# Weight panels signalled in quarters, second output panels begun early, the latent-attention sums moved behind the values

## What is computed

```python
# block 1
h = rmsnorm(x, norm_mix_g); proj = h @ w_in           # many column groups
ya = (sigmoid(mo) * head_rmsnorm(mlstm(...))) @ w_br_m
yb = head_rmsnorm(diff_attention(...)) @ w_br_d
x = x + (sigmoid(g_a) * ya + sigmoid(g_b) * yb) @ w_out
x = x + (gelu(gt) * val) @ w_down                       # val, gt: conv(rmsnorm(x) @ w_up)
x = x + sigmoid(rmsnorm(x) @ w_ple_gate) * (p @ w_ple)
# block 2, layer 0: stick-breaking attention, 16 heads of 64
x = x + (silu(gate) * stick_breaking(q, k, v)) @ l0_w_out
# block 2, layer 1: latent attention, 8 heads of 128 + 64
q, k = rms over 192 (nope | rope) of each head, from a q latent of 256 and a kv latent of 128
x = x + (silu(gate) * causal_softmax(q k^T) v) @ l1_w_out
# block 3: FFN, gated unit | forgetting attention, 8 heads of 64, FFN; modulated by c @ w_ada
y = (norm_a(u * spatial_gate(v)), norm_b(forgetting_attention(...))) @ w_out_3
```

## Time and profile before

| | |
|---|---|
| median of 3 runs | 2626.04 us |
| profiled execution, its own time | 2632.99 us |
| span in the trace | 2631.0 us |
| TensorE busy | 94%, mean granted clock 0.973 |
| VectorE, ScalarE, GpSimd busy | 50%, 39%, 38% |
| DMA | 245.52 MB, mean 93 GB/s |

### The profile page before, as it was taken

How to read it: one execution, slowest core, us unless ns; L and a number is a source line. 1 busy time by engine, 2 the same in 40 slices (tenths; PEclk the granted TensorE clock), 3 DMA queues, 4 the chain that set the end, 5 groups by cost and what they waited for, 6 DMA issues and landing times.

```text
span 2631.0 us, 31263 instructions
## 1 busy us (share of the span) xinstructions
PE 2477.1 (94%) x11720; PEld 1987.5 (76%) x11720; DVE 1324.2 (50%) x1870; ACT 1023.2 (39%) x1327; POOL 1007.3 (38%) x758
## 2 busy tenths in 40 slices
PE   7999899899999899998988899999989989999999
PEld 5887677688887678776766678888869657688886
DVE  6456667866667661444446662222373544522224
ACT  5445576422222543665446542222253433322222
POOL 3332244445554443222443244444424104344442
PEclk9999899999999999999989999999989998999999
DMA  3221496222222122101221122222212102122221
GB/s 137 81 75 54 167 365 261 103 96 96 96 96 96 66 84 75 49 33 50 95 96 64 35 84 96 99 99 98 96 57 93 49 17 80 48 97 96 98 99 57
DMA packets 35957, 245.52 MB, mean 93 GB/s; under 512 B 3951, under 2 KB 4079, under 8 KB 7188
## 3 DMA queue, kind: packets, MB, share of 16 engines
q1 hardware_dynamic: 30096, 207.12, 21.9%
q10 hardware_dynamic: 5764, 37.06, 3.7%
HBM read 242.06 MB, written 2.11 MB: 93 GB/s over the span
## 4 chain that ended last, share of the span: by engine, by line
issue 55%; POOL 28%; PE 15%; DVE 1%; DVEq 0%; POOLq 0%; ACT 0%; ACTq 0%
POOL WL L286 28%; PE PS L316 5%; PE PS L318 5%; PE PS L317 5%; PE PS L1030 0%; PE PS L377 0%; DVE X L2429 0%; DVE ARENA L2424 0%; POOLq L290 0%; DVEq L2095 0%; DVE ARENA L1771 0%; DVEq L2428 0%; PE PS L382 0%; DVE ARENA L1746 0%; POOLq L283 0%
## 5 line engine op out<-in xcount | busy, mean ns | idle before, releaser
L286 POOL TENSOR_TENSOR WL<-WT,WH 128x512 fp32r<-128x512 f32 x754 | 1007.1, 1367 | 1587.9 <-ACT WH L1054 1069.4
L316 PE MATMUL PS<-HH,WH 128*128 128x512 f32 x1568 | 623.2, 397 | 33.8 <-POOL WL L286 10.3
L317 PE MATMUL PS<-HL,WH 128*128 128x512 f32 x1568 | 615.7, 393 | 0.0
L318 PE MATMUL PS<-HH,WL 128*128 128x512 f32 x1568 | 615.6, 393 | 0.0
L1386 ACT CAST WH<-WT 128x2048 fp32r<-128x2048 f32 x90 | 171.9, 1910 | 603.8 <-PE PS L316 603.8
L316 PEld LDWEIGHTS PS<-HH,WH 128*128 128x128 f32 x1568 | 297.7, 190 | 110.4 <-DVE HL L1780 14.6
L316 PE MATMUL PS<-YH,WH 128*128 128x512 f32 x840 | 334.1, 398 | 24.6 <-DVE YL L2559 6.6
L318 PEld LDWEIGHTS PS<-HH,WL 128*128 128x128 f32 x1568 | 297.5, 190 | 63.6
L317 PEld LDWEIGHTS PS<-HL,WH 128*128 128x128 f32 x1568 | 297.9, 190 | 59.6 <-issue 0.2
L318 PE MATMUL PS<-YH,WL 128*128 128x512 f32 x840 | 329.9, 393 | 0.0
L317 PE MATMUL PS<-YL,WH 128*128 128x512 f32 x840 | 329.8, 393 | 0.0
(11 more groups left out here) (305 smaller groups left out, 3350.8 us busy)
## 6 DMA issues: line engine op xcount, KB each, us to landing
WT<-weights SPq DMA_DIRECT2D x188, 1024.0 KB, 4.8
ARENA<-w_ada ACTq DMA_DIRECT2D x33, 1024.0 KB, 6.8
ARENA<-w_ada SPq DMA_DIRECT2D x3, 1024.0 KB, 7.6
X<-x_fm SPq DMA_DIRECT2D x4, 512.0 KB, 7.3
out_fm<-X SPq DMA_DIRECT2D x8, 256.0 KB, 2.1
ARENA<-rel_rows ACTq DMA_DIRECT2D x1, 1024.0 KB, 5.2
CON<-constants SPq DMA_DIRECT2D x1, 640.0 KB, 11.2
WT<-weights SPq DMA_DIRECT2D x1, 512.0 KB, 5.1
```

Of the source, the lines that this page charges most:

```text
L286: i = nc.gpsimd.tensor_tensor(WL[s][:, e], WT[s][:, e], WH[s][:, e].bitcast(F32), ALU.subtract)
L316: i0 = nc.tensor.matmul(o, w[0], r[0], start=first, stop=False, skip_group_check=True)
L317: nc.tensor.matmul(o, w[0], r[1], start=False, stop=False, skip_group_check=True)
L318: i2 = nc.tensor.matmul(o, w[1], r[0], start=False, stop=last, skip_group_check=True)
```

## The change

Four edits in the order of the program.

1. GpSimd signals after each of the four pieces: three times `w_piece`, the last time `w_lo`. In most places outside the feed-forward blocks TensorE opens a panel with `open_pieces` (waits for the cast alone) and waits for a piece in front of the first matmul that reads it. The first matmul of a panel signals `w_used` as before, so the next cast may come earlier. The feed-forward blocks and the panels inside the differential and forgetting attentions keep `open_panel`.
2. The second output panel of the stick-breaking layer (G_OUT2 + 1) and of block 3 (G_OUT4 + 1) is accumulated in PSUM banks that the attention no longer uses (4 and 5; 2 and 3), by `ahead_steps`. ScalarE casts that panel earlier, and VectorE reads these two tiles from there.
3. In latent attention TensorE does `mla_sums` and `mla_spread` behind the values of the turn; ScalarE does `mla_root` behind the copy.
4. VectorE does `mla_keys` at j = 1 and `mla_out` behind tile j = 0, with `mla_diag` in the middle of it.

```diff
@@ GpSimd, low
-                i.then_inc(sem("w_lo"), 1)
+                    i.then_inc(sem("w_lo" if c + PANEL // 4 == width else "w_piece"), 1)
@@ TensorE
+            def open_pieces(g):
+                pe.wait_ge(sem("w_hi"), g + 1)
+                opened.update(g=g, piece=0)
+                return g
+            def piece(g, end):
+                if opened["g"] == g and end > PANEL // 4 * opened["piece"]:
+                    q = (end - 1) // (PANEL // 4)
+                    opened["piece"] = q + 1
+                    if q == 3:
+                        pe.wait_ge(sem("w_lo"), g + 1)
+                    else:
+                        pe.wait_ge(sem("w_piece"), 1 + 3 * (g - 1) + q + 1)
@@ exact3 (part = panel, end column, weights are the moving operand)
                 i0 = nc.tensor.matmul(o, w[0], r[0], start=first, stop=False, skip_group_check=True)
+                if part and part[2]:
+                    piece(part[0], part[1])
                 nc.tensor.matmul(o, w[0], r[1], start=False, stop=False, skip_group_check=True)
+                if part and not part[2]:
+                    piece(part[0], part[1])
                 i2 = nc.tensor.matmul(o, w[1], r[0], start=False, stop=last, skip_group_check=True)
@@ raw_panel, panel_h, v_panel, out_gemm, the third merge panel, G_PLE, G_MLV
-                open_panel(g)
+                open_pieces(g)
@@
+            def ahead_steps(g, c, b, k0, k1, frees=False):
+                for k in range(k0, k1):
+                    i0, i2 = exact3(psb(b), wtile(g % 2, 8, 256, k, c, c + P), (YH[:, k, :], YL[:, k, :]), k == 0, k == DT - 1,
+                                    (g, k * 256 + c + P, False))
+                    if frees and k == k0:
+                        used(g, i0)
+                if k1 == DT:
+                    i2.then_inc(sem("ahead_done"), 1)
@@ stick-breaking, last pair, before the values
+                if p == SB_PAIRS - 1:
+                    open_pieces(G_OUT2 + 1)
+                    pe.wait_ge(sem("sa_ready"), 2 * p + 1)
+                    ahead_steps(G_OUT2 + 1, 0, 4, 0, 2)
@@ and behind them
+            ahead_steps(G_OUT2 + 1, 0, 4, 2, DT - 1)
             for e in range(2):
                 out_step(G_OUT2, (YH, YL), "sy_ready", P * e, ob[e], DT - 1)
-            for g in range(G_OUT2 + 1, G_OUT2 + 4):
-                open_panel(g)
+            ahead_steps(G_OUT2 + 1, 0, 4, DT - 1, DT, frees=True)
+            ahead_steps(G_OUT2 + 1, P, 5, 0, DT)
+            for g in range(G_OUT2 + 2, G_OUT2 + 4):
+                open_pieces(g)
@@ latent attention, TensorE
-                if j == 0 and h + 1 < MLA_HEADS:
-                    mla_sums(h + 1)
-                if j == 1 and h + 1 < MLA_HEADS:
-                    mla_spread(h + 1)
...
                 if v:
                     mla_values(v - 1)
+                if j == 0 and h + 1 < MLA_HEADS:
+                    mla_sums(h + 1)
+                if j == 1 and h + 1 < MLA_HEADS:
+                    mla_spread(h + 1)
@@ block 3, behind gate_sums
+            open_pieces(G_OUT4 + 1)
+            for e in range(2):
+                ahead_steps(G_OUT4 + 1, P * e, 2 + e, 0, 4)
             for e in range(2):
                 for k in range(4, DT):
                     out_step(G_OUT4, (YH, YL), "gy_ready", P * e, ob[e], k)
-            for g in range(G_OUT4 + 1, G_OUT4 + 4):
-                open_panel(g)
+            for e in range(2):
+                ahead_steps(G_OUT4 + 1, P * e, 2 + e, 4, DT, frees=e == 0)
+            for g in range(G_OUT4 + 2, G_OUT4 + 4):
+                open_pieces(g)
@@ ScalarE: the casts of the second output panels
                     nc.scalar.copy(LBH[:, :], LB[e]).then_inc(sem("slh_ready"), 1)
+                    if p == SB_PAIRS - 1 and e == 0:
+                        next_panel(G_OUT2)
...
+                if v == FOX_TILES - 5:
+                    next_panel(G_OUT4)
@@ ScalarE, latent attention
-                if j == 0 and h + 1 < MLA_HEADS:
-                    mla_root(h + 1)
...
                 nc.scalar.copy(PT[:, v % 2, 0:P * (j + 1)], PS[:, 4 + v % 2, 0:P * (j + 1)]).then_inc(sem("pt_ready"), 1)
+                if j == 0 and h + 1 < MLA_HEADS:
+                    mla_root(h + 1)
@@ VectorE, latent attention
-            def mla_out(h):
-                dve.wait_ge(sem("o_ready"), h + 1)
-                tt(LG[:, h, :], psb(6 + h % 2), LG[:, h, :], ALU.mult).then_inc(sem("mlo_read"), 1)
-                dve.drain()
-                split(LG[:, h, :], h, "mly_ready")
+            def mla_out(h, ahead):
+                if h >= 0:
+                    dve.wait_ge(sem("o_ready"), h + 1)
+                    tt(LG[:, h, :], psb(6 + h % 2), LG[:, h, :], ALU.mult).then_inc(sem("mlo_read"), 1)
+                    dve.drain()
+                    nc.vector.tensor_copy(YH[:, h, :], LG[:, h, :])
+                if ahead < MLA_HEADS:
+                    mla_diag(ahead)
+                if h >= 0:
+                    dve.drain()
+                    tt(YL[:, h, :], LG[:, h, :], YH[:, h, :].bitcast(F32), ALU.subtract).then_inc(sem("mly_ready"), 1)
...
-                    if j == 1 and h:
-                        mla_out(h - 1)
-                    if j == 2 and h + 1 < MLA_HEADS:
+                    if j == 1 and h + 1 < MLA_HEADS:
                         mla_keys(h + 1)
                     mla_scale(v + 1)
-                if j == 0 and h + 1 < MLA_HEADS:
-                    mla_diag(h + 1)
+                if j == 0:
+                    mla_out(h - 1, h + 1)
```

More of the change, by code:

```diff
@@ L312, in take, with exact3 @@
                 return b
-            def exact3(o, w, r, first, last):
+            def exact3(o, w, r, first, last, part=None):
                 i0 = nc.tensor.matmul(o, w[0], r[0], start=first, stop=False, skip_group_check=True)
+                if part and part[2]:
+                    piece(part[0], part[1])
                 nc.tensor.matmul(o, w[0], r[1], start=False, stop=False, skip_group_check=True)
+                if part and not part[2]:
+                    piece(part[0], part[1])
                 i2 = nc.tensor.matmul(o, w[1], r[0], start=False, stop=last, skip_group_check=True)
@@ L1141, in normalise, with out_gemm @@
                     n["ru"] += DT - 1
-            def out_gemm(g0, gain):
+            def out_gemm(g0, gain, ahead=False):
                 for q in range(4):
-                    next_panel(g0 + q)
-                    skip(2)
+                    if not (ahead and q == 0):
+                        next_panel(g0 + q)
+                    if not (ahead and q == 1):
+                        skip(2)
                     if q:
@@ L1707, in _ @@
             for q in range(4):
-                next_panel(G_OUT4 + q)
-                skip(2)
+                if q:
+                    next_panel(G_OUT4 + q)
+                if q != 1:
+                    skip(2)
                 if q:
@@ L1804, in trail, with add_out @@
                         n["hh"] += DT
-            def add_out(gain, dst=(HH, HL), meanwhile=None):
+            def add_out(gain, dst=(HH, HL), meanwhile=None, ahead=None):
                 for k in range(DT):
-                    b = take()
-                    free(tt(X[:, k, :], psb(b), X[:, k, :], ALU.add), b)
+                    if ahead and k in (2, 3):
+                        dve.wait_ge(sem("ahead_done"), k - 1)
+                        tt(X[:, k, :], psb(ahead[k - 2]), X[:, k, :], ALU.add)
+                    else:
+                        b = take()
+                        free(tt(X[:, k, :], psb(b), X[:, k, :], ALU.add), b)
                     new()
@@ L2381, in _ @@
             skip(2)
-            mla_rope(1)
+            mla_turn(1)
+            mla_squares(1)
             mla_softmax(0)
@@ L2398, in _ @@
                 if j == 3 and h + 2 < MLA_HEADS:
-                    mla_rope(h + 2)
-            mla_out(MLA_HEADS - 1)
+                    mla_turn(h + 2)
+                    mla_squares(h + 2)
+            mla_out(MLA_HEADS - 1, MLA_HEADS)
             n["att"] = NQ * MLA_HEADS
@@ L2560, in _ @@
             for k in range(DT):
-                b = take()
-                free(nc.vector.tensor_copy(ACC[:, k, :], psb(b)), b)
+                if k in (2, 3):
+                    dve.wait_ge(sem("ahead_done"), k + 1)
+                    nc.vector.tensor_copy(ACC[:, k, :], psb(k))
+                else:
+                    b = take()
+                    free(nc.vector.tensor_copy(ACC[:, k, :], psb(b)), b)
                 new()
```

36 lines of the change are left out of this document (22 added, 14 removed).

## The result

The changed kernel takes 2614.1 us (median of 8 runs, 2612.1 to 2619.2), the kernel before 2626.9 beside it (8 runs, 2624.3 to 2631.7): ratio 0.9946, 95% interval 0.9934 to 0.9958, 12.8 us faster. The forecast was 2598, the range 2583 to 2613: less than half of the 28.1 us came, and the time lies 1.1 us outside the range.

What follows compares the result with a forecast made beforehand. TensorE, busy 94% of the span, was taken as the bound, with only time between its matmuls to win. Terms 5.0 + 1.7 + 1.7 + 7.6 + 9.1 + 3.0 = 28.1 us, from 2626.0, gave 2598; range 2583 to 2613.

Steps and rivals of the forecast that it cites:

- the term for latent attention: Latent attention: new order saves 0.55 us per head, 16.5 instead of 17.04; 3.0 us in all, bounds -4 and 16.
- heads of 17 us or more: Latent attention: a sign that the forecast is wrong; heads of 16.5 us were expected.
- 1.00 where waits stayed under 2 us: Clock reading from stretch 1418 to 1435: granted clock 1.00 with waits under 2 us, 0.51 after 3 us.
- the half clock at 1394: Latent attention near 1394 us: a slow-clock stretch that may go, counted as +1 us.
- Merge: Merge panels from 298.9 and later small waits: GpSimd waits go, DMA landings limit the gain; 5.0 us, bounds 1 and 12.
- PLE gate: PLE gate, 868 to 919: first GpSimd wait (1.6 us) goes, other three give nothing; 1.7 us, bounds -2 and 6.4.
- value panel: Value panel of latent attention: TensorE, free at 1351.1, no longer waits until 1352.8; 1.7 us, bounds 0 and 2.
- Stick-breaking end: End of stick-breaking attention: third output panel starts at 1245.1 instead of 1252.69; 7.6 us, bounds 3 and 8.5.
- Last output product: Last output product: 24 second-panel matmuls fill the 6.6 us wait, third panel starts at 2184.4; 9.1 us, bounds 6 and 9.5.
- the second: Rival: gain from pieces goes back to DMA landings and VectorE, latent attention loses; 2609 to 2617 us, chance 0.22.
- The first (all waits go whole): Rival across all changed places: every named wait vanishes entirely; 54 us, 2572, chance 0.10.
- The third (weight loads exposed inside a triple): Rival in newly opened panels: waits before the third weight load expose it; costs 39 us, 2637, chance 0.03.

Runs made afterwards that it cites:

- second pair: The kernel before and the changed kernel, each unaltered and profiled once more: 2630.5 and 2616.1 us.
- experiment 3: Changed kernel with VectorE alone back in its old order: 2606.7 us; with TensorE and ScalarE alone back in theirs: 2625.0 us.
- the quarters alone: Kernel before plus only the signals after each of GpSimd's four subtraction pieces and panels opened by them: 2621.7 us, ratio 0.9979.
- the order that held 1.00 at each entry tried: Changed kernel, VectorE in old order but adding squares before the rope product: 2606.5 us; with twelve fill matmuls 2604.3; entered 1.4 us later 2610.4.

## Why the prediction was wrong

**The failed step** is the term for latent attention: "1.03 less 0.5 is 0.55 per head, 16.5 instead of 17.04 [...] Sum 3.0. Bounds -4". It measured -7.8 and -9.9, 11 to 13 us off, and below its own bound; the whole sum missed by 13.7 in the second pair. The sum put the clock of the new order at nothing: it took a head's saving at 1.00 six times. In its place the clock's part of the stage grew by 11.9 and 15.0 us (6.8 to 18.8, 5.1 to 20.2), while the rest fell by 4.1 and 5.2, more than forecast. More in part because waits shrink beside slow matmuls: in one trace of experiment 3 a slow stretch of 3.4 us makes a head of 16.55 us into 17.73, 1.2 more, though half of 3.4 is 1.7. The forecast named heads of 17 us or more as a sign that it was wrong, and they take 17.7.

The reason given for a full clock was "1.00 where waits stayed under 2 us", read from the stretch 1418 to 1435 in the earlier trace rows, where waits of 1.5 and 0.9 us stand. The trace of before itself had a head with the same waits (1.6 and 0.8 us) and another clock:

```profile
1382.28:1400.99 18.71, 16.29 (x91) 13.08 (x90) 11.22 (x26) 11.46 (x21) 5.19 (x4) 0.91 0.18 57
```

The forecast counted this stretch ("the half clock at 1394") only as something to win. With six matmuls ahead of the stage the same code has 0.83 in a head with the same waits. So the 17.04 us was a good case that the forecast took for the rule. Two things are shown: the old order keeps or loses the clock by its entry, and the new order lost it at every entry tried, the good one of before among them.

The warning of the Trainium skill, TensorE: Matmul & The Clock Gate, section HAM oscillation — how this bites in real kernels, that idle gaps bring the slow clock, was weighed for two places only. The trace agrees in the first latent head, where 10.2 us at half clock stand around and behind a wait of 3.5 us. It doesn't say which order is worse: between 1435.08 and 1452.12 TensorE stood idle 2.4 us in the old order at 1.00, and 1.0 us in a head of the new one at 0.90, where slow matmuls fill part of the waits. Why the clock falls in the new order stays open: no run here settles which arrangement of waits and one-column sums brings it.

**Merge**, 5.0: got 2.6 and 4.2, 3.4 of either being the clock of one stretch. The first merge wait went, and the fourth panel came 39.8 us behind the stage's start; the forecast had 38.5. The reason given is the one seen, though it wasn't tried by an experiment; timeline of the changed kernel, ScalarE, VectorE, and the panel that waits:

```profile
302.02 1.03 ACT L1094 ACTIVATE PS<-ARENA 128x1024 f32<-128x1024 f32 x1 [5.21 <-DMA ARENA<-rows]
...
318.72 0.50 PE L332 MATMUL PS<-YH,WH 128*128 128x512 f32 x1 [1.98 <-DVE ARENA L2128]
...
319.99 1.22 DVE L2103 TENSOR_TENSOR ARENA<-ARENA,PS 128x1024 f32<-128x1024 f32 x1 [1.33 <-DMA ARENA<-w_ada]
321.13 0.68 DVE L2122 TENSOR_TENSOR ARENA<-PS,ARENA 128x512 f32<-128x512 f32 x1
321.96 0.47 PE L332 MATMUL PS<-HH,WH 128*128 128x512 f32 x1 [0.19 <-DVE ARENA L2122]
```

ScalarE and VectorE sit at the landings of the earlier trace rows; the one at 319.99 comes before the gating that frees the bank, a step the forecast left out. Up to there the stage gained 2.0 and 2.6 us of the 3.3 forecast, behind it 0.6 and 1.6 of 1.7.

**PLE gate and value panel**, 1.7 each: 2.7 and 2.6, in the second pair 2.9 and 2.3. The wait for the sum became 8.2 us, forecast 8.5.

**Stick-breaking end**, 7.6: 7.7 and 8.0, step by step as forecast. Timeline: the subtraction that meets GpSimd (2.07 us, forecast 1.49 + 0.7), the values, the first matmul behind them, and the third output panel, 13.3 us behind the values' start; before it was 21.6:

```profile
1218.73 2.07 DVE L2346 TENSOR_TENSOR LBL<-ARENA,LBH 128x1280 fp32r<-128x1280 f32 x1 [1.82 <-PE PS L811]
...
1223.85 2.38 PE L826 MATMUL PS<-ARENA 128*64 128x512 f32 x16
1226.15 0.50 PE L332 MATMUL PS<-YH,WH 128*128 128x512 f32 x1
...
1237.17 0.39 PE L332 MATMUL PS<-YH,WH 128*128 128x512 f32 x1
```

**Last output product**, 9.1: 8.6 and 7.1; the second pair has 5.1 instead of 6.8 us of clock to win back. The third panel starts at 2172.58, 48.3 us behind the first, instead of 56.8.

**Rivals.** The time lies in the span of the second (2609 to 2617, chance 0.22), and half of its mechanism is right: latent attention loses. The other half is not: the quarters alone kept 6.3 us in the medians. The first (all waits go whole) falls with the 8.2 us before the sum. The third (weight loads exposed inside a triple) is refuted by the steps of 0.68 us in the new panels.

## What to carry to other kernels

In this kernel a granted clock of 1.00 over a stretch with waits belonged to the moment of entry as much as to the code. So look for other heads of the same stage with another clock first, put a microsecond of work ahead of the stage before you trust it, and price every edit ahead of it by that difference too. Compare orders at equal clock, by the clean head, and then ask separately what each loses to the clock. Here the order that held 1.00 at each entry tried was worth more than one whose stage is 3 us shorter without the clock's part and didn't hold it.

## What the runs showed of the hardware that was not expected

- In the kernel before, six matmuls, 1.4 us, ahead of the stage raised the median by 12 us; in the trace one wait of 1.8 us is new in the stage, and the heads behind it, with unchanged waits, run at 0.91 and 0.83.
- Heads of one order come in steps: 17.04, 18.7 and 20.35 us at 1.00, 0.91 and 0.83 of the clock.
- Edits don't add: alone they change the median by -6.3, +1.8 and +9.7 us, together by -12.8. With the same kernel around it and at about the same entry the new order of latent attention costs 18.8 us of clock, the old one 5.1 to 6.8.
- The quarters alone vary most, from 2612.8 to 2636.5 us, where the latent edits alone stay within 7.3.
